# Two ScalarE steps of an attention moved back by one place each: a logarithm and an exponential of the stick-breaking tiles

## The reference

```
a  (4 heads): indexed attention, the best 64 keys per query are chosen, then softmax
b  (4 heads): stick-breaking
     z = q.k * scale                      (strictly causal)
     log_keep = log_sigmoid(-z)
     log_between = reversed cumsum(log_keep) - log_keep
     weight = exp(log_sigmoid(z) + log_between)
c  (8 heads): softmax in a window of 128 with a sink, in two groups of 4: c0, c1
out = concat(oa, ob, oc) -> rms norm per head -> @ w_o
```

## Time and profile before

| | before |
|---|---|
| median of 3 runs | 2307.69 us |
| the profiled execution's own time | 2305.76 us |
| its span | 2304.0 us |
| TensorE matmul busy | 2215.7 us, 96% |
| VectorE busy | 1315.1 us, 57% |
| ScalarE busy | 1113.8 us, 48% |
| GpSimd busy | 763.9 us, 33% |
| mean DMA rate | 143 GB/s |

### The profile page before, as it was taken

The page is one execution under the profiler, slowest core; times in us unless marked ns, Lnnn a source line. Parts: engine busy times, 40 slices in busy tenths (PEclk is TensorE's granted clock), DMA queues, the critical chain, the costliest instruction groups (busy, mean ns, idle before and its releaser), DMA issues.

```text
span 2304.0 us, 41122 instructions
## 1 busy us (share of the span) xinstructions
PE 2215.7 (96%) x14780; PEld 1931.6 (84%) x14780; DVE 1315.1 (57%) x2274; ACT 1113.8 (48%) x2324; POOL 763.9 (33%) x563
## 2 busy tenths in 40 slices
PE   7999998999999999999999999999989999999998
PEld 4869997868998798878888679888879999787998
DVE  3768999676446735541343764363455564437663
ACT  3565554564555435442363653233343565647553
POOL 2406874513654221122321012222213235221443
PEclk9999999999999999999999999999999999999999
DMA  8666998676766222223222112223323335222554
GB/s 302 223 238 216 322 315 290 206 259 224 223 184 197 88 83 64 65 73 91 83 65 83 37 47 89 94 66 99 93 72 115 105 115 170 82 83 65 170 164 141
DMA packets 159781, 328.47 MB, mean 143 GB/s; under 512 B 17696, under 2 KB 21024, under 8 KB 159520
## 3 DMA queue, kind: packets, MB, share of 16 engines
q1 hardware_dynamic: 159504, 325.80, 44.1%
q0 software_dynamic: 144, 0.85, 0.1%
HBM read 325.53 MB, written 1.05 MB: 142 GB/s over the span
## 4 chain that ended last, share of the span: by engine, by line
PE 67%; issue 14%; DVE 9%; POOL 5%; ACT 2%; DMA 2%; SPq 1%; POOLq 0%; ACTq 0%; DVEq 0%
PE PS L1846 13%; PE PS L1847 13%; PE PS L1848 13%; PE PS L1891 4%; PE PS L1893 4%; PE PS L1892 4%; POOL WL L1763 4%; DVE WORK L2521 3%; DVE WL L2419 2%; PE PS L729 2%; PE PS L709 1%; POOL AR L1783 1%; PE PS L743 1%; PE PS L745 1%; PE PS L744 1%
## 5 line engine op out<-in xcount | busy, mean ns | idle before, releaser
L1763 POOL TENSOR_TENSOR WL<-RAW,WH 128x512 fp32r<-128x512 f32 x434 | 615.6, 1421 | 1445.5 <-ACT WH L2158 1293.8
L1846 PE MATMUL PS<-AR,WH 128*128 128x256 f32 (+1 forms) x2632 | 858.2, 326 | 3.3 <-DVE AR L1614 2.0
L1847 PE MATMUL PS<-AR,WH 128*128 128x256 f32 (+1 forms) x2632 | 844.4, 321 | 0.0
L1848 PE MATMUL PS<-AR,WL 128*128 128x256 f32 (+1 forms) x2632 | 844.4, 321 | 0.0
L2158 ACT ACTIVATE WH<-RAW 128x512 fp32r<-128x512 f32 x840 | 492.6, 626 | 318.8 <-PE PS L1848 175.1
L2419 DVE TENSOR_TENSOR WL<-RAW,WH 128x512 fp32r<-128x512 f32 x434 | 379.3, 874 | 436.8 <-ACT WH L2158 435.5
L1846 PEld LDWEIGHTS PS<-AR,WH 128*128 128x128 f32 x2632 | 497.1, 189 | 58.3 <-issue 10.9
L1847 PEld LDWEIGHTS PS<-AR,WH 128*128 128x128 f32 x2632 | 497.1, 189 | 40.7 <-issue 2.4
L1848 PEld LDWEIGHTS PS<-AR,WL 128*128 128x128 f32 x2632 | 496.9, 189 | 39.7
L1891 PE MATMUL PS<-WH,AR 128*128 128x256 f32 x768 | 219.5, 286 | 0.0
L1893 PE MATMUL PS<-WH,AR 128*128 128x256 f32 x768 | 216.5, 282 | 0.0
(11 more groups left out here) (310 smaller groups left out, 3098.8 us busy)
## 6 DMA issues: line engine op xcount, KB each, us to landing
RAW<-stream SPq DMA_DIRECT2D x868, 256.0 KB, 3.0
WORK<-mods SPq DMA_DIRECT2D x144, 512.0 KB, 5.8
WORK<-stream SPq DMA_DIRECT2D x68, 256.0 KB, 4.8
C<-consts SPq DMA_DIRECT2D x1, 1088.0 KB, 7.4
XX<-xT SPq DMA_DIRECT2D x1, 1024.0 KB, 10.1
XX<-ctxT SPq DMA_DIRECT2D x1, 1024.0 KB, 6.0
outT<-XX SPq DMA_DIRECT2D x1, 1024.0 KB, 4.8
C<-consts POOLq DMA_DIRECT2D x1, 832.0 KB, 7.6
```

The source lines that it names most:

```text
L1763: pool.tensor_tensor(WL[:, u % 4, cut, :], raw(u, 1), WH[:, u % 4, cut, :].bitcast(f32), ALU.subtract).then_inc(lo_done[1], 1)
L1846: pe.matmul(out, WH[:, u % 4, k, :], moving[:, 0, k, :], start=(k == 0), stop=False)
L1847: pe.matmul(out, WH[:, u % 4, k, :], moving[:, 1, k, :], start=False, stop=False)
L1848: last = pe.matmul(out, WL[:, u % 4, k, :], moving[:, 0, k, :], start=False, stop=(k == KC - 1))
```

## The change

`stick_logs(n)` is cut in two: `stick_powers(n)` holds the wait, the absolute value and the first exponential, and `stick_logs(n)` the logarithm. For n = 1 the logarithm now comes after `exps("c0", 0)`. And `stick_exps(0)` comes after `exps("c0", 1)` instead of ahead of `turned_copy(0)`. Both hold in each of the two layers. No instruction is added or removed, and no other engine's program changes.

```diff
--- before.py
+++ after.py
@@ -2281,13 +2281,17 @@
                                           accum_out=COL[:, c + 8 + p:c + 9 + p])
                 last.then_inc(exped, 1)
 
-            def stick_logs(n):
+            def stick_powers(n):
 
                 dst = PRX[n][:, :, 0:P * (n + 1)]
                 act.wait_ge(stick_read, 2 * l + n + 1)
                 chain(act.activation(dst, SM[:, n, :, 0:P * (n + 1)], ACT.Abs))
                 chain.wait()
                 chain(act.activation(dst, dst, ACT.Exp, scale=-1.0))
+
+            def stick_logs(n):
+
+                dst = PRX[n][:, :, 0:P * (n + 1)]
                 chain.wait()
                 act.activation(dst, dst, ACT.Ln, bias=EPSC[:, 1:2]).then_inc(bl, 1)
 
@@ -2321,12 +2325,14 @@
                 act.activation(OT[:, n, at:at + 4, :], PS[:, 6, 0:T].rearrange("p (a b) -> p a b", a=4), ACT.Copy)
                 act.activation(SQO[i % 4], PS[:, 6, 0:T], ACT.Square).then_inc(o_read, 1)
 
+            stick_powers(0)
             stick_logs(0)
+            stick_powers(1)
+            exps("c0", 0)
             stick_logs(1)
-            exps("c0", 0)
-            stick_exps(0)
             turned_copy(0)
             exps("c0", 1)
+            stick_exps(0)
             turned_copy(1)
             heads_out(0)
             stick_exps(1)
```

## The result

The changed kernel took 2311.32 us (median of 12 runs, 2309.34 to 2315.57), the kernel before in the same measurement 2308.24 us (12 runs, 2300.39 to 2313.36). The ratio of the two sets of runs is 1.0021 with a 95% interval of 1.0012 to 1.0029: 0.21% slower, some 5 us by the ratio (the two medians lie 3.1 us apart), and clear of no change. The time lies inside the predicted range, but the forecast was "the same" with 95%, and the mechanism that made it slower had 4%.

What follows compares the result with a forecast made beforehand. TensorE, busy 96%, was taken as the bound, the attention one TensorE chain from turn(2), held by ScalarE's turned_copy(1). Order 1.4 plus clock 1.1 us made 2.5, on the median 2307.69: 2310.2 us, range 2307.6 to 2312.3.

Steps and rivals of the forecast that it cites:

- the same: Whole kernel: a time within about 0.2%, 4.6 us, of the kernel before, given 95%.
- the mechanism that made it slower: Attention: the long TensorE pause gives two low-clock stretches in a row in each layer, 2314.0 us; chance 4%.
- The path: Attention: late stick exponential starts turn(1) at 482.50, not 480.54, after one TensorE pause of 3.05 us.
- The logarithm at no cost: ScalarE: the logarithm of n = 1 ends at 479.05, VectorE needs it at 480.15, so nothing of VectorE moves.
- The shift of 0.7 us a layer: Attention: turn(2) starts 0.74 us later and the shift reaches L2113, 0.7 us a layer, ends 0.3 and 0.9.
- The clock's term: Second layer's attention also falls to the lower clock after the pause, at 1.1 us, ends 0 and 1.6.
- the order: Both attentions: ScalarE's new order delays turn(2) and what follows, two layers at 0.7 us, +1.4 us.
- The second layer keeps its full clock: Rival, second layer's attention: the clock stays at 1.00 despite the longer pause, 2309.1 us; chance 36%.
- Two low stretches in a row in each layer: Rival, attention: two low stretches per layer instead of one in one layer, 6.3 us with the shift; chance 4%.
- 0.2% as the bound of what can be told: Whole kernel: a measurement can tell about 0.2%, 4.6 us, from no change.

Runs made afterwards that it cites:

- e1_log: Only the logarithm of n = 1 moved back, the stick exponential of n = 0 left in place, against the kernel before: ratio 0.9998 (0.9987 to 1.0010).
- e4_fill: The whole change plus twelve matmuls that nobody reads ahead of turn(1), against the kernel before: ratio 1.0000 (0.9990 to 1.0010).
- e2_exp: Only the stick exponential of n = 0 moved back, the logarithm of n = 1 left in place, against the kernel before: ratio 1.0029 (1.0017 to 1.0041).
- e3_weigh: The whole change plus weigh(0) moved ahead of turn(1) on TensorE, against the kernel before: ratio 1.0019 (1.0009 to 1.0029).
- e10_before: The kernel before, unchanged, timed against itself and profiled again: ratio 1.0006 (0.9996 to 1.0016).
- e7_fill4: The whole change plus four matmuls that nobody reads ahead of turn(1), against the kernel before: ratio 1.0011 (1.0002 to 1.0020).

## Why the prediction was right and wrong

- *The path* was right: the stick exponential late, turn(1) and all behind it late, one pause in place of two. It was 2.80 us long (482.35 to 485.15) where I had 3.05.
- *The logarithm at no cost* was right, by its distances and by `e1_log`. VectorE was not touched.
- *The shift of 0.7 us a layer* failed twice. It was 0.26 us at turn(2) (`e4_fill`). Four distances of my sum were too long: from the second power to the sink's exponential 0.96 us and not 1.09, from the sink's exponential to the logarithm 1.84 and not 1.94, from the logarithm to turned_copy(0) 1.04 and not 1.20, and from turn(1) to turned_copy(1) 0.69 and not 0.79. Together that is the 0.48 us between 0.74 and 0.26, to a rounding. The second and third come of adding ends where the next instruction starts before the end on record. The last was a misreading: the 0.16 us from turn(0)'s end to turned_copy(0) were not TensorE's to ScalarE, since that copy stood behind the stick exponential of 479.28; where a copy waits for TensorE it comes 0.03 us behind it. And I took TensorE, busy without a gap in the earlier trace rows, for one chain. It is not: VectorE's maxima set the exponentials of c1/0, and behind them heads_out(1) releases weigh(2), so that by turn(7) 0 to 0.1 us were left.
- *The clock's term* is the step that failed and that decided. I had one low stretch more, in the second layer, at 1.1 us, and the first layer as it was. Measured are 6.8 us at the lower clock in five of eight layers and 3.4 in two, against 3.4 in two of six. The price was off too: by turn(7) 3.4 us cost 1.4 to 1.6 us (33.65 to 33.84 against 32.28) and 6.8 us cost 2.8 to 3.1 (35.12 to 35.40). The 1.06 us that I took, from the distances to L2113, had the scatter of the DMA in it (9.96 us from turn(7) to L2113 in the one layer, 10.39 in the other); the 1.63 us that I kept as the other end was the nearer one. In the sum of 2.5 us the order stood with 1.4 and has at most 0.2 for both layers, the clock stood with 1.1 and has some 4.0. That the time still fell into the range is in part luck: one term was too large by 1.2 us while the other was too small by 2.9. (The upper end of the range adds up to 2312.2 us, not 2312.3; nothing hangs on it.)
- *The rivals.* "The second layer keeps its full clock" was seen in one profile of four. "Two low stretches in a row in each layer" was the mechanism in two profiles of four and in half of a third. I gave it 4% and called it unlikely because the clock had come back after 3.4 us of work at half speed in the earlier trace rows; that speaks of a clock that falls while TensorE works, and the long pause lets it fall while TensorE stands. Its price of 6.3 us was too high by the order's 1.4 us (by turn(7) the first profiles of before and after are 1.75 + 3.11 = 4.9 us apart), and it does not come in every run, which is how 0.2% came out and not 0.3%.
- The Trainium skill, "TensorE: Matmul & The Clock Gate", section "What's actually happening", says of a kernel's start that the number of slow matmuls varies between runs of one kernel. These traces agree, here in the middle of a kernel: 13.6, 3.4, 10.2 and 13.6 us at the lower clock in the attentions of four executions of one kernel. I should have averaged over it, in both kernels, and not read one trace as the rule for each layer.
- *0.2% as the bound of what can be told.* Two sets of 12 runs, against 12 and 23 of before, gave intervals of about 0.17% in width, so a loss of 0.2% is told from none.

## What to carry to other kernels

Here a step off the busiest engine's path could be moved for nearly nothing until it joined two short pauses of TensorE into one; then the granted clock had the price, not the order. So look at both. Check such a suspicion by filling the pause with matmuls that nobody reads: if the time comes back with the order unchanged, as in `e4_fill`, it was the clock. And take the clock's state from several profiles, since one execution shows one draw.

## What the runs showed that I had not expected

When the clock fell before turn(1), 9.3 to 10.3 us from L2288 with TensorE standing (five layers of the changed kernel, two of `e2_exp`, one of `e3_weigh`), it stayed low for 6.8 us; when it fell at 11.6 to 12.5 us, with TensorE at work again (two layers of the changed kernel, one of `e3_weigh`, one of before), for 3.4 us. Nothing in between was seen. What sets the moment of the fall was not tried.

In `e10_before` 3.4 us at the lower clock cost nothing: they lay at 7.7 to 11.1 us, behind a pause of 2.07 us, turn(2) came at 11.50 and turn(7) at 32.28 us all the same, because TensorE was waiting for ScalarE there anyway. The same 3.4 us from about turn(2) on cost 1.4 to 1.6 us.

Four matmuls, 1.04 us of work in the pause, left the clock up in both profiled layers (`e7_fill4`), while weigh(0), 1.0 us of work in the same pause, left it to fall in both (`e3_weigh`), in one of them inside the pause and in the other only after turn(2) had begun. With one profile of each, and timed ratios of 1.0011 and 1.0019 whose intervals overlap, this stays open.
